# Hybrid encoder step: an opening in single products, two gather slots exchanged, three picks moved, and a top-16 without casts

## The reference

```
h = rmsnorm(x);  q_a, k_a, v_a, q_i, k_i, w_i, q_b, k_b, v_b, g_b = split(h @ w_in)
score = sum_h w_i[h] * relu(q_i[h] . k_i)          # index scores
keep the top 64 (prompt) or 132 (streams) keys; softmax attention over them
retention heads with a carried state; x = x + concat(attention, retention) @ w_out
h2 = rmsnorm(x)
q = (h2 @ w_query) per head, two halves of 128     # 8 heads
v1, i1 = top16(q1 . keys1);  v2, i2 = top16(q2 . keys2)
cand = v1[:, None] + v2[None, :];  top_s, sel = top16(cand)      # of 256 pairs
e = i1[sel // 16] * 128 + i2[sel % 16];  gate = softmax(top_s)
x = x + sum over heads and 16 picks: gate * gelu(exp_u[e] . h2) * exp_v[e]
y = rmsnorm(x)
```

## Time and profile before

| | |
|---|---|
| median of 3 runs | 1144.43 us (1144.29 to 1145.9) |
| the profiled execution, whole / span | 1144.88 / 1143.1 us |
| PE busy | 856.5 us (75%) |
| DVE busy | 784.8 us (69%) |
| POOL busy | 536.3 us (47%) |
| ACT busy | 454.8 us (40%) |
| DMA packets | 456.60 MB, mean 399 GB/s |

### The profile page before, as it was taken

How to read it: one execution, slowest core, us unless ns; L and a number is a source line. 1 busy time by engine, 2 the same in 40 slices (tenths; PEclk the granted TensorE clock), 3 DMA queues, 4 the chain that set the end, 5 groups by cost and what they waited for, 6 DMA issues and landing times.

```text
span 1143.1 us, 12068 instructions
## 1 busy us (share of the span) xinstructions
PE 856.5 (75%) x3879; PEld 396.3 (35%) x3884; DVE 784.8 (69%) x2005; ACT 454.8 (40%) x1423; POOL 536.3 (47%) x437
## 2 busy tenths in 40 slices
PE   8999988997896858685686777587666756655555
PEld 6748743443232424241243442143223222211111
DVE  2325877876677888796666786757877777667554
ACT  2121454333444334552564663343343333333334
POOL 0002445553555554553553553556564654455442
PEclk9999999999999888897889898889898788887879
DMA  9902999999999999999999999999999999999996
GB/s 375 411 2 70 421 425 425 427 424 430 425 427 425 426 428 426 361 430 422 425 427 425 425 427 427 425 426 427 426 427 426 427 427 428 427 425 427 427 428 269
DMA packets 66791, 456.60 MB, mean 399 GB/s; under 512 B 8227, under 2 KB 10019, under 8 KB 15526
## 3 DMA queue, kind: packets, MB, share of 16 engines
q0 software_dynamic: 55888, 402.68, 83.8%
q1 hardware_dynamic: 10694, 52.87, 11.4%
q10 hardware_dynamic: 144, 0.26, 0.1%
HBM read 451.49 MB, written 3.24 MB: 398 GB/s over the span
## 4 chain that ended last, share of the span: by engine, by line
DMA 48%; PE 26%; DVE 11%; POOL 7%; ACT 4%; issue 3%; SPq 0%; POOLq 0%; DVEq 0%
DMA rows<-in_uv,ids 37%; PE ps L598 25%; DMA wt<-in_uv,ids 8%; DVE rows L2043 6%; POOL rows L537 4%; POOL work L520 2%; DMA wt<-in_uv,last_ids 1%; DMA rows<-in_w_qi 1%; ACT work L1249 1%; ACT wt L1249 1%; DMA wt<-in_w_q 1%; ACT wgt L1249 1%; DVE wt L2043 1%; PE ps L601 1%; ACT zact L1249 1%
## 5 line engine op out<-in xcount | busy, mean ns | idle before, releaser
L537 POOL DMA_INDIRECT rows<-in_uv,ids x352 | 400.3, 1137 | 444.9 <-PE ps L598 360.7
L598 PE MATMUL ps<-rows,work 128*64 128x512 f32 x1416 | 409.4, 707 | 245.2 <-ACT work L1249 239.7
L2043 DVE CUSTOM_DVE_ANT_0 rows<-rows,wt 128x1024 f32<-128x1024 f32 x226 | 276.9, 1225 | 160.9 <-DMA rows<-in_uv,ids 155.7
L1249 ACT ACTIVATE zact<-zdot 128x1 f32<-128x1 f32 x354 | 71.6, 202 | 488.2 <-DVE zdot L2043 480.5
L598 PEld LDWEIGHTS ps<-rows,work 128*64 128x64 f32 x1416 | 96.2, 151 | 479.3 <-ACT work L1249 327.3
L598 PE MATMUL ps<-wt 128*128 128x128 f32 (+6 forms) x719 | 195.9, 476 | 30.4 <-ACT wt L1249 28.1
L2043 DVE CUSTOM_DVE_ANT_0 rows<-rows,masks 128x1024 f32<-128x1024 f32 x128 | 156.3, 1224 | 67.3 <-DMA rows<-in_uv,ids 64.5
L598 PEld LDWEIGHTS ps<-wt 128*128 128x128 f32 (+2 forms) x724 | 97.8, 185 | 106.6 <-issue 58.8
L1249 ACT ACTIVATE work<-pair,wgt 128x64 f32<-128x64 f32 x354 | 123.4, 349 | 11.5
L1249 ACT ACTIVATE wgt<-zact,gates 128x1 f32<-128x1 f32 x354 | 104.5, 295 | 11.6
L598 PEld LDWEIGHTS ps<-work,wt 128*128 128x128 f32 (+1 forms) x664 | 84.2, 202 | 48.6 <-issue 48.2
(11 more groups left out here) (178 smaller groups left out, 722.9 us busy)
## 6 DMA issues: line engine op xcount, KB each, us to landing
wt<-in_w_q SPq DMA_DIRECT2D x7, 2048.0 KB, 15.9
rows<-in_uv,ids POOLq DMA_INDIRECT x352
rows<-in_w_out SPq DMA_DIRECT2D x2, 2048.0 KB, 32.5
wt<-in_w_out SPq DMA_DIRECT2D x2, 2048.0 KB, 12.0
wt<-in_ckv SPq DMA_DIRECT2D x16, 256.0 KB
x<-in_x SPq DMA_DIRECT2D x5, 512.0 KB, 8.9
rows<-in_w_qi SPq DMA_DIRECT2D x1, 2048.0 KB, 13.3
wt<-in_w_qa SPq DMA_DIRECT2D x1, 2048.0 KB, 12.5
```

The lines of the kernel that those rows point to most:

```text
L537: pool.indirect_dma_start(row[s], None, a["uv"], bass.IndirectOffsetOnAxis(ap=ids[:, own(n // KP).start + n % KP:own(n // KP).start + n % ...
L598: return nc.tensor.matmul(out, lhsT, rhs, start=start, stop=stop)
L1249: return nc.scalar.activation(*args, **kw)
L2043: V.tensor_tensor_reduce(row[s][:, 0:D], row[s][:, 0:D], h2r[t][:, n % 2, :], 1.0, 0.0, ALU.mult, ALU.add, zdots[s]).then_inc(dotted, 1)
```

## The change

Six things are changed together.

1. `index_queries` counts single products, so that the transposes and the queries of unit 0 stand between fewer of them. `h2_t(0)` is cut into two halves (`h2_t0`) that wait for the halves of h2; the wait for the square of x (`sqd`) moves from PE to the readers of the transposes. Unit 0's ids are spread as soon as they exist, ahead of its gates (`spread_first`), and `picked` counts one more.
2. Slots 4, 5 and slots 6, 7 exchange places: picks 4 and 5 now wait for `q_ps` 2 and picks 6 and 7 for `qi_ps` 3. On PE `query(1)` stands ahead of most of tile 2's index products.
3. `y_start(0)` goes from the opening to pick 14. The first `add_experts` starts the bank instead.
4. The queries of unit 3 are at pick 14 (10 before), those of unit 4 at 22 (20 before).
5. Attention and retention of tile 1 stand some 2 to 4 picks later; half of the top-64 of tile 1 (`score_round`) is put between picks 0 to 4 instead of ahead of pick 0.
6. The top-16 loses its two casts to float and two shifts or masks; ids and ranks stay integers, the table `iota` holds two ramps (0, 16, 32, ... and 0, 1, 2, ...), one reduction over both halves replaces a reduction and a multiply-add.

```diff
-        PLACE = (4, 5, 6, 7, 0, 1, 2, 3)
+        PLACE = (4, 5, 6, 7, 2, 3, 0, 1)
...
-            return {2: 8, 3: 10, 4: 20, 7: 72, 8: 88, ...
+            return {2: 8, 3: 14, 4: 22, 7: 72, 8: 88, ...
...
                 if n == 4:
+                    pool.wait_ge(q_ps, 2)
+                if n == 6:
                     pool.wait_ge(qi_ps, 3)
-                if n == 6:
-                    pool.wait_ge(q_ps, 2)
...
+            def spread_first():
+                pe.wait_ge(q_sb, 1)
+                for k in range(2):
+                    pe.wait_ge(chosen, k + 1)
+                    for j in range(2):
+                        for q in range(2):
+                            last = mm(spread_psum(k)[64 * q:64 * q + 64, j * KP + k * 8:j * KP + k * 8 + 8], ...
+                    last.then_inc(spread_ps, 1)
...
-            index_queries(1, 6, 0, 1)
-            h2_t(0)
-            index_queries(1, 6, 1, 2)
+            h2_t0(0)
+            index_queries(1, 6, 0, 3)
+            h2_t0(1)
+            index_queries(1, 6, 3, 7)
             query(0)
-            index_queries(1, 6, 2, 3)
+            index_queries(1, 6, 7, 9)
             query_scores(0)
-            index_queries(1, 6, 3, 4)
+            index_queries(1, 6, 9, 32)
             pe.wait_ge(gb_sb, 1)
-            index_queries(2, 7, 0, 1)
+            index_queries(2, 7, 0, 4)
...
             sums_1(0)
+            spread_first()
             dots_1(3)
             sums_1(1)
-            spread_out(0)
             sums_1(2)
             sums_1(3)
-            index_queries(2, 7, 1, 4)
             query(1)
+            index_queries(2, 7, 4, 24)
+            query_scores(1)
+            index_queries(2, 7, 24, 32)
             later_qa(0)
-            query_scores(1)
             pe.wait_ge(qi_sb, 3)
-            y_start(0)
             add_experts(0)
...
             relu_1(3)
+            take_q(1)
             later_qi()
-            take_q(1)
...
-                then(V.tensor_copy(topf, topi))
...
-                V.tensor_scalar(rank[:, 0, :], besti, 4, None, ALU.logical_shift_right)
-                then(V.tensor_scalar(rank[:, 1, :], besti, 15, None, ALU.bitwise_and))
-                yield from across(V.tensor_copy(rankf, rank))
+                yield from across(V.tensor_tensor(rank, besti..., nibble..., ALU.bitwise_and))
...
-                yield from across(V.tensor_reduce(half_id, hot, AX.X, ALU.add))
-                V.scalar_tensor_tensor(flat[u % 2][:, 0, :], half_id[:, 0, :], float(NK), half_id[:, 1, :], ALU.mult, ALU.add).then_inc(chain, 1)
+                ids_of = V.tensor_reduce(flat[u % 2][:, 0, :], hot.rearrange("p e k r -> p k e r"), AX.XY, ALU.add)
```

More of the change, by code:

```diff
@@ L628, in keys_values, with index_queries @@
                 natural(t, w_kv, 6 + t % 2, NKV).then_inc(kv_ps, 1)
[L630 to L635, removed]
+            def index_queries(t, bank, i0, i1):
+                for i in range(i0, i1):
+                    j, c = divmod(i, KC)
+                    last = mm(ps[:, bank, j * P:(j + 1) * P], w_qi[:, c, j * P:(j + 1) * P], hT(t, c), c == 0, c == KC - 1)
+                if i1 == 4 * KC:
                     last.then_inc(qi_ps, 1)
@@ L787, in scores_1, with h2_t0 @@
                 last.then_inc(sc_ps, 1)
-            def h2_t(t):
[L790 to L794, removed]
+            def h2_t0(e):
+                pe.wait_ge(gained, e + 1)
+                for c in range(4 * e, 4 * e + 4):
+                    last = tr(ps[:, 3 * e, (c % 4) * P:(c % 4 + 1) * P], h2[:, c * P:(c + 1) * P])
+                if e:
+                    last.then_inc(h2t_ps, 1)
+            def h2_t(t):
+                pe.wait_ge(hready, TILES + t + 1)
                 if t == 1:
@@ L814, in query_part @@
                     if u == 1:
[L815 removed]
+                        pe.wait_ge(picked, 2)
                     k = q_load(u)
@@ L986, in retention_1 @@
             def retention_1():
-                yield from until(26)
+                yield from until(28)
                 pe.wait_ge(rotated, 2)
@@ L1384, in natural @@
             def natural():
-                for start, dst, t, bank, s, done, func in ((33, vb, 1, 3, vb_ps, vb_sb, ACT.Copy), (39, vb, 2, 2, vb_ps, vb_sb, ACT.Copy),
+                for start, dst, t, bank, s, done, func in ((34, vb, 1, 3, vb_ps, vb_sb, ACT.Copy), (39, vb, 2, 2, vb_ps, vb_sb, ACT.Copy),
                                                            (45, gs, 1, 3, gb_ps, gb_sb, ACT.Silu), (57, gs, 2, 3, gb_ps, gb_sb, ACT.Silu)):
@@ L1617, in across, with post @@
                 dve.wait_ge(s, n)
+            def post(ins, s):
+                key = s.name
+                count[key] = count.get(key, 0) + 1
+                ins.then_inc(s, 1)
+                yield
             def bank4(bank):
@@ L1752, in top16_pairs @@
                                                   top[:, 1:2, :].broadcast_to([P, KP, KP]), ALU.add))
-                then(V.max(out=best[:, 0:8], in_=cand))
+                V.max(out=best[:, 0:8], in_=cand).then_inc(chain, 1)
+                V.tensor_scalar(topi[:, 0, :], topi[:, 0, :], 7, None, ALU.logical_shift_left).then_inc(chain, 1)
+                count[chain.name] += 2
+                dve.wait_ge(chain, count[chain.name])
                 yield from across(V.match_replace(out=cand2, in_to_replace=best[:, 0:8], in_values=cand, imm_value=TAKEN))
@@ L1818, in _ @@
             then(V.memset(ident_bf[:], 0.0), blank)
+            for i, bits in enumerate((240, 15)):
+                ins = V.memset(nibble[:, i:i + 1], bits)
+            then(ins)
             first_norm(0)
@@ L1906, in retention_1 @@
             def retention_1():
-                yield from until(23)
+                yield from until(25)
                 dve.wait_ge(cs_again, 16)
```

113 lines of the change are left out of this document (65 added, 48 removed).

## The result

| | before | with the change |
|---|---|---|
| median | 1144.98 us (1144.29 to 1145.9, 4 runs) | 1159.07 us (1157.69 to 1162.23, 4 runs) |
| ratio | | 1.0126, 95% interval 1.0102 to 1.015 |
| the profiled execution, whole / span | 1144.88 / 1143.1 us | 1162.23 / 1160.4 us |

The change makes the kernel 1.3% slower, 14 us, and the prediction (1144.4, range to 1147.4) was wrong. The profiled execution is the longest of the four, 3.2 us above their median, so its rows overstate the loss a little.

What follows compares the result with a forecast made beforehand. Time was the start of the pick stream, plus bytes at the full DMA rate, plus stretches with too little to do. +0.2 (opening) + 0.2 (pick 23) - 0.4 (loss at 461) = 0.0 gave 1144.4 us, range 1141.9 to 1147.4.

Steps and rivals of the forecast that it cites:

- the full rate: Whole pick stream: DMA engines move 426 GB/s when busy, read from 172 to 442 us of the kernel before.
- 426 GB/s from 175 on: Sign in the profile after: the steady DMA rate from 175 us on would be 426 GB/s.
- The start of the stream: Opening: query(0) and the spread come earlier, pick 0 is asked for at 107.0, stream starts 2.7 us earlier.
- What PE releases: Opening to 142 us: PE waits 1.7 us for ACT, first add 0.7 us later; opening net 0.2 us later.
- DMA shares under 0.9: Sign for 120 to 142 us: the prediction is wrong if no slice there falls under 0.9.
- Picks 8 to 23: Stretch behind the opening: moved work covered, stream just empty at pick 23 near 174.7, charged 0.2 us.
- the third rival: query(2) late: weights land after 12 us, PE at half clock; +3.5 us, 1147.9 us, chance 0.16.
- a new hole beyond 150: Sign of being wrong: a new hole in the DMA stream opening beyond 150 us.
- The table load: ACT's load before the first Gelu: 1.28 us; a rival had 1.4 us more, 1145.8 us, chance 0.04.
- The new top-16: Top-16 in the opening: fewer casts and shifts make it 0.4 us shorter, with DVE ready before PE.
- the loss at 461: DMA loss from 461 to 482 us, where DVE waits for rstd: 0.4 us taken off, bounds nothing and 1.8.

Runs made afterwards that it cites:

- e1: Changed kernel plus 64 unused bytes a partition where iota stood, so rows is at its old address 32512: 1147.06 us, ratio 1.0022.
- e2: Kernel before with iota declared behind rows, so rows alone begins 64 bytes lower at 32448: 1157.2 us, ratio 1.0108.
- e5: e4 with ACT weighing picks 0 and 1 ahead of later_qi: 1142.54 us, ratio 0.9984 against the kernel before.
- e4: e1 with unit 3's queries and y_start(0) at pick 10, unit 4's queries at pick 20: 1145.41 us, ratio 1.0008 against the kernel before.
- e9: e5 with unit 3's and 4's queries back at picks 14 and 22 (late load): 1143.3 us, ratio 0.9995 against the kernel before.
- e7: Kernel before with the new top-16 alone and 64 bytes left for iota: 1143.64 us, ratio 0.9988.
- e3: Kernel before with m16 and iota declared behind rows, so rows begins 128 bytes lower at 32384: 1155.79 us, ratio 1.0105.
- e8: Kernel before with 256 bytes of small tensors moved behind the large ones, rows at 32256: 1145.02 us, ratio 1.0004.
- e12: e9 run once more, the same kernel, for a second trace: 1147.59 us, one run, no ratio.
- e10: e5 with the old top-16 of the kernel before: 1144.81 us, ratio 1.0001 against the kernel before.
- e11: Kernel before with rows at 32256, a multiple of 256, but wt and what follows off 256: 1145.41 us, ratio 1.0007.

## Why the prediction was wrong

- **The step that failed** is in the first part: the time is "the moment at which the stream of picks starts, plus the bytes at the full rate", and the full rate was taken over as 426 GB/s. For the changed kernel it is 421, for a reason in the diff that I didn't cost at all: the removed declaration of `iota` moves `rows` off a multiple of 256 bytes. It is 12.0 of the 14 us (e1), and 12.6 in the kernel before (e2). Neither the forecast nor any rival had it. The prediction did ask for 426 GB/s from 175 on, which is the line that shows it.
- The start of the stream was right: `query(0)` 90.92 (forecast 90.85), the spread 106.24 (106.0), pick 0 at 107.17 (107.0), 2.5 us earlier than before.
- What PE releases was right: the first add at 126.33 behind 1.72 us of waiting for ACT (126.2 and 1.7), pick 8 at 128.54 (128.4), the weights asked for at 140.92 (140.8). That this wait takes the gain away is shown by removing it: e5 has 407 GB/s from 112 to 142 us instead of e4's 380, which is 1.9 us, and e9 is 3.1 us faster than e1. DMA shares under 0.9 came where they were forecast (0.88 from 128 to 132 us).
- Picks 8 to 23 were mis-sized. I charged 0.2 us, and the third rival (0.16) is what the trace shows: landing after 11.3 us, then half the clock in a part of `query(2)`, with unit 4's load at 179.0 instead of 174, and pick 23 asked for at 176.66, active some 1.5 us later, instead of active at 174.7. In e1 this stretch costs 3.4 us, by the table. The prediction had named "a new hole beyond 150" as a sign of being wrong, and the hole at 177 to 179 is one.
- The table load costs its 1.28 us and nothing more: the Gelu starts 0.01 us behind it at 124.47. The drain of some 1380 ns that the Trainium skill gives with it (ScalarE: Activation LUTs, What ACT_TABLE_LOAD costs) shows neither here nor in e5.
- The new top-16 was under-sized: 0.4 us in the sum, where it stood for the loss at 461, and 1.2 measured alone; 0.5 us are an earlier start in e7's trace, and that it shortens the loss at 461 isn't shown. Its masking costs 0.19 us, and its sum over two dimensions 0.69, within the bounds that I gave them.
- With the address put right the time is 1147.06: inside the range, and near the third rival's 1147.9 rather than the forecast. So without the address the range would have held, but not by the forecast's own sum.

## What to carry to other kernels

In a kernel that moves large rows at the full rate of the DMA, the SBUF address of the region they land in is part of the design: keep it on a multiple of 256 bytes, and print the addresses after every added or removed declaration, however small. When a trace shows a lower rate at a full DMA share, look at the transfers themselves before looking for a wait. And a request that is released earlier is worth what the next engine's list lets through: here a table load and a copy on ACT used up 2.5 us of an earlier start, until two small weighings were put ahead of them.

## What was unexpected of the hardware

- 8 KB rows gathered to a region that starts 192 or 128 bytes above a multiple of 256 move at 421 GB/s instead of 426, with a DMA share of 1.01 in both cases; a start that is moved by a whole 256 bytes is free (e2, e3, e8).
- The same load of 2.10 MB, asked for at the same place of the program among the same picks, landed 8.1 us after the request in e5, and 10.7 and 11.2 us after it in e9 and e12. These kernels are the same up to pick 10.
- PE did `query(2)` in 3.81 us after waits of 0.17 to 1.49 us (before, e3, e5 to e8, e10, e11) and in 5.44 to 6.73 after waits of 2.14 to 3.44 (the changed kernel, e1, e2, e4, e9, e12). The granted clock from 150 to 156 us, at 1.00 in the kernel before, was 0.79 in the changed one, a mean over both levels:

```profile
150.00:156.00 6.00, 3.74 (x23) 3.77 (x24) 2.58 (x6) 0.00 (x0) 1.49 (x2) 0.79 1.01 425
```
